# Interleaving the blocks of a recurrent mixer, and moving the head projections of an attention loop

## The chip, the cores and the metric

The kernel runs on the 8 cores of one Trainium2 chip. Each core runs the same program on its own 1024 tokens; the cores do not exchange data. The time is that of the slowest core, in microseconds (us) on the device. A core has a matrix engine (TensorE, PE in the profile), a vector engine (VectorE, DVE), an engine for activation functions (ScalarE, ACT), a general engine (GpSimd, POOL) and a queue engine (SyncE, SP). Each engine works through its own queue in program order, and waits for the others by semaphores.

## The reference

Two trunk layers of a diffusion backbone. The two parts that matter here are the recurrent half of the mixer of layer 0 and the attention of layer 1, cut to what is computed:

```
def rglru_dir(x, wa, ba, wi, bi, lam, h0, reverse):
    r = sigmoid(einsum('blnh,nhk->blnk', xb, wa) + ba)
    i = sigmoid(einsum('blnh,nhk->blnk', xb, wi) + bi)
    log_a = -LRU_C * r * softplus(-lam)
    a = exp(log_a)
    mult = sqrt(-expm1(2.0 * log_a))
    return linear_scan(a, mult * (i * x), h0, reverse)

# even_mixer, its recurrent half
gate, x_b = split(ub, 2)
xc = dwconv(x_b, lru_conv_w, 2, 1) + lru_conv_b
hf = rglru_dir(xc, ..., h0f, False)
hb = rglru_dir(xc, ..., h0b, True)
y_b = (hf + hb) * gelu(gate)

# attend, for each of 8 heads
s = einsum('bqhd,bkhd->bhqk', qi, k) * scale
p = softmax(s)
o = einsum('bhqk,bkhd->bqhd', p, v)
```

## The kernel before

Everything is held feature-major: 128 features on the partitions, the core's 1024 tokens along the free axis, mostly as two halves of 512 (`hh`), which is what one PSUM bank holds in float32. The kernel is written out in order; a small recording layer (`K.op`, `K.mm`, `K.dma`) keeps for every tile the last writer and the readers, and puts a semaphore wait in front of an instruction where one is needed. Nothing reorders: the order of the code is the order of every engine's queue. All matmuls are recorded by one helper and so carry one line, L159; `K.bank()` hands out the eight PSUM banks in rotation and skips those in `K.reserved`. Weights come through `ring`, six slots of SBUF; the loads are issued by POOL (L193).

**The recurrent stage** (L578 to L676) loops over eight blocks `j` of 128 channels. One block is a chain:

- F, the front: `proj` runs 16 matmuls for the gate `gg` and 16 for the input `xb`; ScalarE copies `xb` to `U4` (L589); a tanh form of GELU goes back and forth between ScalarE and VectorE (L594, L595, L597, L599, L600); then a convolution of four taps into `xc`, the first on ScalarE (L604), three on VectorE (L608) and four small corrections (L612); ScalarE writes `xc` out as bf16 `xcb` and halved as `xch` (L618, L619).
- G, the gates: 8 matmuls of `xcb` with `wa` and `wi`, for two directions and two halves, each read by a tanh on ScalarE (L631) into `thr` and `thi`.
- B, the back: for both directions two exponentials of `thr` on ScalarE (L637, L639), two cheap VectorE steps (L643, L645), a Ln and an Exp on ScalarE, which make the square root (L649, L650), two products and a correction on VectorE (L655, L656, L659), a scan (L663 forward, L668 backward), the sum of both and the product with the gate (L674, L675), and two small copies on POOL (L666, L671).

At `j` = 0 and `j` = 4 two weight tiles are loaded, for four blocks each. The tiles `thr`, `thi`, `av`, `a2` and `hd` have one buffer per direction, `U4`, `xc` and `xcb` one, `gl` and `xch` two. ScalarE keeps one table of functions at a time: Tanh and Exp before Ln share one, Ln and the Exp behind it another, and the change between them is an `ACT_TABLE_LOAD`.

**The attention loop** (from L1046) runs over 8 heads. A head begins with 24 matmuls that project its queries and keys (18 from `cqn`, 6 from `ckva`), which ScalarE copies out as `qn` (L1050) and `kn` (L1064) and VectorE turns into `qr` (L1056 to L1058). Then, for each half `hh`, a loop over 12 key tiles: two matmuls for the scores, an Exp on ScalarE into `pT` (L1079), one matmul with `v` and one with ones. The scores go to banks 4 to 7, three tiles ahead. The results lie in banks 0 and 1 for `hh` = 0 and in banks 2 and 3 for `hh` = 1, and are divided on VectorE (L1085, L1086), which sets the banks free.

Of the kernel before, what the change touches and what calls it, by code (L numbers as in the profile page):

```python
# [14 lines left out]
T = 1024  # L15
# [241 lines left out]
def build(stage=99, debug=False):  # L257
# [320 lines left out]
    for j in range(8 if stage >= 3 else 0):  # L578
        if j % 4 == 0:
            pG = ring.load(wview(w_in0, 0, 8, 1536 + (j // 4) * 512, 512), 8, 512)  # L580
            pX = ring.load(wview(w_in0, 0, 8, 2560 + (j // 4) * 512, 512), 8, 512)
# [3 lines left out]
        if not getattr(U, "zeroed", False):  # L585
            K.op(pool, lambda h, U=U: h.memset(U.t[:], 0.0), w=(U,))
            U.zeroed = True
        for hh in range(2):
            K.op(act, lambda h, hh=hh, U=U: h.activation(out=U.t[:, 2 + hh * 512:2 + (hh + 1) * 512], in_=xb[hh].t[:], func=AF.Copy),  # L589
                 r=(xb[hh],), w=(U,))  # L590
        gl = rotbuf("gl", 2, [128, T], F32, MX)
        for hh in range(2):
            sq = rotbuf("gsq", 1, [128, 512], F32, MX)
            K.op(act, lambda h, hh=hh, sq=sq: h.activation(out=sq.t[:], in_=gg[hh].t[:], func=AF.Square), r=(gg[hh],), w=(sq,))  # L594
            K.op(dve, lambda h, sq=sq: h.tensor_scalar(out=sq.t[:], in0=sq.t[:], scalar1=0.044715, scalar2=1.0, op0=ALU.mult, op1=ALU.add),  # L595
                 r=(sq,), w=(sq,))
# [14 lines left out]
        for (ocol, ucol, k) in ((256, 256, 0), (256, 257, 1), (257, 257, 0), (255, 258, 3)):
# [3 lines left out]
                 r=(U, nlcw, xc), w=(xc,))  # L615
        xcb = rotbuf("xcb", 1, [128, T], BF16, MX)
        xch = rotbuf("xch", 2, [128, T], F32, MX)
        K.op(act, lambda h, xc=xc, xcb=xcb: h.activation(out=xcb.t[:], in_=xc.t[:], func=AF.Copy), r=(xc,), w=(xcb,))  # L618
        K.op(act, lambda h, xc=xc, xch=xch: h.activation(out=xch.t[:], in_=xc.t[:], func=AF.Copy, scale=0.5), r=(xc,), w=(xch,))  # L619
        thr_ = [rotbuf("thr", 2, [128, T], F32, MX) for _ in range(2)]  # L620
        thi_ = [rotbuf("thi", 2, [128, T], F32, MX) for _ in range(2)]
        av_ = [rotbuf("av", 2, [128, T], F32, MX) for _ in range(2)]
        a2_ = [rotbuf("a2", 2, [128, T], F32, MX) for _ in range(2)]
        hd_l = [rotbuf("hd", 2, [128, T], F32, MX) for _ in range(2)]
        for d in range(2):
            dj = d * 8 + j
            for (wt, th, hbias) in ((wa, thr_[d], hba), (wi, thi_[d], hbi)):
                for hh in range(2):
# [4 lines left out]
                         r=(b, hbias), w=(th,))  # L633
        for d in range(2):
            dj = d * 8 + j
            thr, av, a2 = thr_[d], av_[d], a2_[d]
            K.op(act, lambda h, thr=thr, av=av, dj=dj: h.activation(out=av.t[:], in_=thr.t[:], func=AF.Exp, bias=m4.t[:, dj:dj + 1], scale=m4.t[:, dj:dj + 1]),  # L637
                 r=(thr, m4), w=(av,))
            K.op(act, lambda h, thr=thr, a2=a2, dj=dj: h.activation(out=a2.t[:], in_=thr.t[:], func=AF.Exp, bias=m8.t[:, dj:dj + 1], scale=m8.t[:, dj:dj + 1]),  # L639
                 r=(thr, m8), w=(a2,))  # L640
        for d in range(2):
            a2 = a2_[d]
            K.op(dve, lambda h, a2=a2: h.tensor_scalar(out=a2.t[:], in0=a2.t[:], scalar1=-1.0, scalar2=1.0, op0=ALU.mult, op1=ALU.add),  # L643
                 r=(a2,), w=(a2,))
            K.op(dve, lambda h, a2=a2: h.tensor_scalar(out=a2.t[:], in0=a2.t[:], scalar1=1e-30, scalar2=None, op0=ALU.max),  # L645
                 r=(a2,), w=(a2,))
        for d in range(2):
            a2 = a2_[d]
            K.op(act, lambda h, a2=a2: h.activation(out=a2.t[:], in_=a2.t[:], func=AF.Ln), r=(a2,), w=(a2,))  # L649
            K.op(act, lambda h, a2=a2: h.activation(out=a2.t[:], in_=a2.t[:], func=AF.Exp, scale=0.5), r=(a2,), w=(a2,))  # L650
        hdir = []
        for d in range(2):
            dj = d * 8 + j
            thi, av, a2, hd = thi_[d], av_[d], a2_[d], hd_l[d]
            K.op(dve, lambda h, a2=a2, xch=xch: h.tensor_tensor(out=a2.t[:], in0=a2.t[:], in1=xch.t[:], op=ALU.mult), r=(a2, xch), w=(a2,))  # L655
            K.op(dve, lambda h, a2=a2, thi=thi: h.scalar_tensor_tensor(out=a2.t[:], in0=thi.t[:], scalar=1.0, op0=ALU.add, in1=a2.t[:], op1=ALU.mult),  # L656
                 r=(a2, thi), w=(a2,))
            c0 = 256 if d == 0 else 255
            K.op(dve, lambda h, av=av, c0=c0: h.tensor_scalar(out=av.t[:, c0:c0 + 513:256], in0=av.t[:, c0:c0 + 513:256], scalar1=flags.t[:, 2:3],  # L659
                                                            scalar2=None, op0=ALU.mult),  # L660
                 r=(av, flags), w=(av,))
            if d == 0:
                K.op(dve, lambda h, av=av, a2=a2, hd=hd, dj=dj: h.tensor_tensor_scan(out=hd.t[:], data0=av.t[:], data1=a2.t[:], initial=h0.t[:, dj:dj + 1],  # L663
                                                                             op0=ALU.mult, op1=ALU.add),
                     r=(av, a2, h0), w=(hd,))
                K.op(pool, lambda h, hd=hd: h.tensor_copy(out=lru_out.t[:, j * 4:(j + 1) * 4], in_=hd.t[:, 255:1024:256]), r=(hd,), w=(lru_out,))  # L666
            else:
                K.op(dve, lambda h, av=av, a2=a2, hd=hd, dj=dj: h.tensor_tensor_scan(out=hd.t[:, ::-1], data0=av.t[:, ::-1], data1=a2.t[:, ::-1],  # L668
                                                                             initial=h0.t[:, dj:dj + 1], op0=ALU.mult, op1=ALU.add),
                     r=(av, a2, h0), w=(hd,))  # L670
                K.op(pool, lambda h, hd=hd: h.tensor_copy(out=lru_out.t[:, 32 + j * 4:32 + (j + 1) * 4], in_=hd.t[:, 0:1024:256]), r=(hd,), w=(lru_out,))  # L671
# [698 lines left out]
```

How the kernel before makes its waits and increments, by code:

```python
    def _waits(self, e, need):  # L119
        for s, v in need.items():
            if e.is_pe and s == e.sem:
                continue
            if e.known.get(s, 0) >= v:
                continue
            e.h.wait_ge(self.sems[s], v)
            e.known[s] = v
# [10 lines left out]
    def op(self, e, fn, r=(), w=(), inc=True):  # L137
        self._waits(e, self._need(r, w))
        ins = fn(e.h)
        if inc:
            e.n += 1
            ins.then_inc(self.sems[e.sem], 1)
            ev = (e.sem, e.n)
        else:
            ev = (e.sem, e.n + 1)
        for t in w:
            t.w = [ev]
            t.r = []
        for t in r:
            self._addr(t, ev)
        return ins
# [57 lines left out]
    def barrier(self):  # L209
        for e in self.engs:
            for f in self.engs:
                if f is e or f.n == 0:
                    continue
                if e.known.get(f.sem, 0) < f.n:
                    e.h.wait_ge(self.sems[f.sem], f.n)
                    e.known[f.sem] = f.n
            for ds in self.dma_sems:
                if e.known.get(ds[0], 0) < ds[1]:
                    e.h.wait_ge(self.sems[ds[0]], ds[1])
                    e.known[ds[0]] = ds[1]
# [1 line left out]
    def finish(self):  # L222
        sp = self.sp
        for f in self.engs:
            if f is sp or f.n == 0:
                continue
            if sp.known.get(f.sem, 0) < f.n:
                sp.h.wait_ge(self.sems[f.sem], f.n)
        for ds in self.dma_sems:
            sp.h.wait_ge(self.sems[ds[0]], ds[1])
        self.es.close()
```

The softmax here doesn't subtract the row's maximum and nothing guards it: scores larger than these inputs give would overflow.

## Time and profile before

| | |
|---|---|
| median of 4 runs | 2883.37 us |
| the profiled execution | 2883.13 us |
| its span on the slowest core, core 0 | 2882.1 us |
| spans of the 8 cores | 2852.6 to 2882.1 us |
| PE busy | 2049.6 us, 71% |
| VectorE busy | 1045.9 us, 36% |
| ScalarE busy | 749.5 us, 26% |
| POOL busy | 168.3 us, 6% |

The table is read so: the span runs from the first instruction to the last, and the profiled execution takes 1.0 us more than it. The shares are means over stages of quite different kind; the recurrent stage lies at 185 to 568 us of the span, the attention loop at 1565 to 1818 us. Between them are the output projection, the dense feed-forward part and the long convolution, behind them the experts.

### The profile page before, as it was taken

The page shows a single profiled execution, that of the slowest core. Times are in us where ns is not written, and L with a number is a line of the kernel's source. Part 1 is how long each engine was busy: PE and PEld are TensorE (multiplying, and loading weights), DVE is VectorE, ACT ScalarE, POOL GpSimd, SP SyncE. Part 2 cuts the span into 40 slices and gives each one's busy share as a digit, 9 for nine tenths or more (in the row PEclk, how much of TensorE's full clock was granted, in tenths as well). Part 3 has the DMA queues.
Part 4 walks back from the last instruction along what each step waited for, and adds up shares of the span by engine and source line. Part 5 has one row for each costly group of instructions (what it writes and reads, how often), then busy time and mean ns, then how long its engine had stood idle before and what let it go on. Part 6 is the DMA issues. An engine that isn't in the chain of part 4 may idle for free.

```text
span 2882.1 us, 27603 instructions; the slowest of 8 cores (2852.6 to 2882.1 us)
## 1 busy us (share of the span) xinstructions
PE 2049.6 (71%) x9394; PEld 883.9 (31%) x9394; DVE 1045.9 (36%) x1460; ACT 749.5 (26%) x1150; POOL 168.3 (6%) x183
## 2 busy tenths in 40 slices
PE   1442222166788944467775888859999999999997
PEld 0221010022233411222222333314444444444443
DVE  1125535532122222455552343234333333343333
ACT  3115544432201044411113555151001011011011
POOL 0100000100001000000000000000000000000000
PEclk9676565587899967778887999979999999999998
DMA  6950020037155923202212000353654564745631
GB/s 118 132 74 0 0 29 0 8 37 117 35 91 79 131 43 59 80 26 70 73 44 45 1 1 1 45 81 50 91 81 60 81 85 57 101 59 82 90 52 59
DMA packets 199176, 170.64 MB, mean 59 GB/s; under 512 B 14091, under 2 KB 184843, under 8 KB 199040
## 3 DMA queue, kind: packets, MB, share of 16 engines
q0 software_dynamic: 176128, 133.70, 33.5%
q1 hardware_dynamic: 22912, 35.18, 3.7%
q8 instruction: 79, 1.29, 0.2%
q14 instruction: 57, 0.47, 0.1%
HBM read 297.02 MB, written 5.54 MB: 105 GB/s over the span
## 4 chain that ended last, share of the span: by engine, by line
PE 62%; DVE 13%; ACT 9%; DMA 8%; issue 6%; POOL 1%; DVEq 0%; ACTq 0%; POOLq 0%; SPq 0%
PE bank L159 62%; DMA ring<-l_w_mod 4%; DMA ring<-l_w_in 2%; DVE xc L608 1%; DVE cvh L919 1%; DVE rec L1085 1%; ACT h L461 1%; DVE Ys L989 1%; DVE sp L987 1%; DVE sp L986 1%; DVE sp L995 1%; DVE a L656 1%; DVE a L655 1%; DVE sp L994 1%; DVE hd L668 1%
## 5 line engine op out<-in xcount | busy, mean ns | idle before, releaser
L159 PE MATMUL bank<-h,ring 128*128 128x512 bf16 (+1 forms) x4400 | 1006.3, 392 | 189.1 <-DMA ring<-l_w_in 138.1
L159 PEld LDWEIGHTS bank<-h,ring 128*128 128x128 bf16 (+1 forms) x4400 | 439.2, 101 | 750.5 <-issue 271.1
L159 PE MATMUL bank<-actt,ring 128*128 128x512 bf16 x1760 | 384.2, 381 | 0.0
L775 ACT ACTIVATE sgt<-bank 128x512 f32<-128x512 f32 x220 | 131.3, 597 | 634.2 <-PE bank L159 634.1
L780 DVE TENSOR_TENSOR sgt<-sgt,bank 128x512 f32<-128x512 f32 x176 | 121.1, 688 | 363.9 <-PE bank L159 363.9
L159 PEld LDWEIGHTS bank<-actt,ring 128*128 128x128 bf16 x1760 | 172.9, 98 | 209.4 <-issue 3.9
L797 DVE SCALAR_TENSOR_TENSOR x<-bank,mod,x 128x512 f32<-128x512 f32 x160 | 120.1, 751 | 259.9 <-PE bank L159 259.9
L159 PE MATMUL bank<-ring,Ys 128*128 128x512 bf16 x512 | 136.9, 414 | 83.6 <-DVE Ys L989 35.9
L159 PE MATMUL bank<-ymix,ring 128*128 128x512 bf16 x640 | 144.3, 389 | 56.9 <-DMA ring<-l_w_out 48.5
L159 PE MATMUL bank<-xcb,wa 128*128 128x512 bf16 x32 | 16.6, 621 | 220.9 <-ACT xcb L618 220.9
L782 DVE TENSOR_TENSOR actt<-sgt,bg 128x512 bf16<-128x512 f32 x176 | 121.9, 692 | 18.7 <-DVE sgt L780 0.5
L1079 ACT ACTIVATE pT<-bank 128x512 bf16<-128x512 f32 x192 | 109.7, 599 | 54.1 <-PE bank L159 52.3
L159 PEld LDWEIGHTS bank<-ymix,ring 128*128 128x128 bf16 x640 | 63.7, 100 | 137.1 <-issue 65.3
L1085 DVE RECIPROCAL rec<-bank 128x512 f32<-128x512 f32 x16 | 53.7, 3357 | 137.7 <-PE bank L159 137.7
L159 PEld LDWEIGHTS bank<-ring,Ys 128*128 128x128 bf16 x512 | 52.1, 102 | 167.9 <-issue 119.6
L777 DVE TENSOR_TENSOR actt<-sgt,bank 128x512 bf16<-128x512 f32 x44 | 30.3, 688 | 190.5 <-PE bank L159 186.7
L443 ACT ACTIVATE sq<-x 128x512 bf16<-128x512 f32 x64 | 35.1, 616 | 208.4 <-PE bank L159 86.7
L1143 ACT ACTIVATE bg<-bank 128x512 bf16<-128x512 f32 x16 | 9.6, 597 | 289.3 <-PE bank L159 288.5
L159 PE MATMUL bank<-qn,kn 128*128 128x512 bf16 x192 | 73.5, 383 | 11.5 <-ACT kn L1064 9.8
L159 PE MATMUL bank<-sq,ones_bf 128*128 128x512 bf16 x90 | 41.7, 515 | 55.7 <-ACT sq L443 32.3
L159 PE MATMUL bank<-qr,kr_all 128*128 128x512 bf16 x192 | 73.5, 383 | 0.8 <-DVE qr L1058 0.8
L159 PEld LDWEIGHTS bank<-xcb,wa 128*128 128x128 bf16 x32 | 3.5, 127 | 229.1 <-issue 229.1
(211 smaller groups left out, 1735.6 us busy)
## 6 DMA issues: line engine op xcount, KB each, us to landing
ring<-l_w_mod POOLq DMA_DIRECT2D x24, 1024.0 KB, 21.0
ring<-l_exp_down POOLq DMA_DIRECT2D x32, 704.0 KB, 7.4
ring<-iFm SPq DMA_DIRECT2D x16, 1024.0 KB, 7.6
ring<-l_exp_gate POOLq DMA_DIRECT2D x16, 1024.0 KB, 8.7
ring<-l_exp_up POOLq DMA_DIRECT2D x16, 1024.0 KB, 10.9
ring<-l_w_in POOLq DMA_DIRECT2D x11, 1024.0 KB, 17.0
ring<-l_w_out POOLq DMA_DIRECT2D x8, 768.0 KB, 14.1
ring<-l_exp_gate POOLq DMA_DIRECT2D x8, 768.0 KB, 7.0
```

Source lines behind the costliest of these rows:

```text
L159: ins = e.h.matmul(out_ap, lhsT, rhs, start=start, stop=stop)
L443: K.op(act, lambda h, c=c, sq=sq: h.activation(out=sq.t[:], in_=X(c, hh), func=AF.Square), r=(xh[c][hh],), w=(sq,))
L461: K.op(act, lambda h, c=c, tmp=tmp, o_ap=o_ap, sh=sh: h.activation(out=o_ap, in_=tmp.t[:], func=AF.Identity, bias=sh, scale=gs_ap(c)), r=( ...
L608: K.op(dve, lambda h, k=k, U=U, xc=xc: h.scalar_tensor_tensor(out=xc.t[:], in0=U.t[:, k:k + T], scalar=lcw.t[:, 8 * k + j:8 * k + j + 1], ...
L655: K.op(dve, lambda h, a2=a2, xch=xch: h.tensor_tensor(out=a2.t[:], in0=a2.t[:], in1=xch.t[:], op=ALU.mult), r=(a2, xch), w=(a2,))
L775: K.op(act, lambda h, hh=hh, sgt=sgt: h.activation(out=sgt.t[:], in_=bgk[hh].t[:], func=AF.Silu), r=(bgk[hh],), w=(sgt,))
L777: K.op(dve, lambda h, hh=hh, sgt=sgt, jj=jj: h.tensor_tensor(out=actt[jj].t[:, HS[hh]], in0=sgt.t[:], in1=buk[hh].t[:], op=ALU.mult), r=(s ...
L780: K.op(dve, lambda h, hh=hh, sgt=sgt: h.tensor_tensor(out=sgt.t[:], in0=sgt.t[:], in1=buk[hh].t[:], op=ALU.mult), r=(sgt, buk[hh]), w=(sgt,))
L782: K.op(dve, lambda h, hh=hh, sgt=sgt, jj=jj: h.tensor_tensor(out=actt[jj].t[:, HS[hh]], in0=sgt.t[:], in1=bg.t[:, HS[hh]], op=ALU.mult), r ...
L797: K.op(dve, lambda h, b=b, oc=oc, hh=hh: h.scalar_tensor_tensor(out=X(oc, hh), in0=b.t[:], scalar=gate_ap(oc), op0=ALU.mult, in1=X(oc, hh) ...
L1079: K.op(act, lambda h, sbk=sbk, pT=pT: h.activation(out=pT.t[:], in_=sbk.t[:], func=AF.Exp, scale=SC), r=(sbk,), w=(pT,))
L1085: K.op(dve, lambda h, rec=rec, db=db: h.reciprocal(out=rec.t[:], in_=db.t[:]), r=(db,), w=(rec,))
```

## The change

Both loops are written out in another order.

In the recurrent stage the body of the loop becomes three functions, `lru_F`, `lru_G` and `lru_B`. `lru_F` and `lru_B` are generators that stop after each recorded instruction; `zipper` takes two steps of F of block `j+1` for each step of B of block `j`, and the rest of B follows when F has ended. Then the gates G of block `j+1` come as one piece. In B every instruction of 1024 columns is split into two of 512, each with its own dependences (`halves`); a scan's second half starts from the last column of the first. F keeps its lengths. All four weight tiles of the stage are loaded at `j` = 0 and held.

In the attention loop the projections become `head_proj`; head 0's come ahead of the loop, and those of head `hd_+1` are recorded in the middle of head `hd_`, behind the key loop of `hh` = 0 and ahead of its division. Meanwhile banks 0 and 1 are reserved.

```diff
-    for j in range(8 if stage >= 3 else 0):
-        if j % 4 == 0:
-            pG = ring.load(wview(w_in0, 0, 8, 1536 + (j // 4) * 512, 512), 8, 512)
-            pX = ring.load(wview(w_in0, 0, 8, 2560 + (j // 4) * 512, 512), 8, 512)
+    pst = {}
+
+    def halves(X):
+        if not hasattr(X, "hv"):
+            X.hv = [Tl(X.t, X.name + "_h0"), Tl(X.t, X.name + "_h1")]
+        return X.hv
+
+    def lru_F(j, out):
+        if j == 0:
+            for h4 in range(2):
+                for k_, c_ in (("pG", 1536), ("pX", 2560)):
+                    pst[k_ + str(h4)] = ring.load(wview(w_in0, 0, 8, c_ + h4 * 512, 512), 8, 512, hold=True)
+        pG, pX = pst["pG%d" % (j // 4)], pst["pX%d" % (j // 4)]
         gg = proj(pG[1], pG[0], (j % 4) * 128)
...
+        out.update({"xcb": xcb, "xch": xch, "gl": gl})
+        yield
+
+    def lru_G(j, st):
+        xcb = st["xcb"]
...
-            K.op(act, lambda h, thr=thr, av=av, dj=dj: h.activation(out=av.t[:], in_=thr.t[:], func=AF.Exp, bias=m4.t[:, dj:dj + 1], scale=m4.t[:, dj:dj + 1]),
-                 r=(thr, m4), w=(av,))
+            for hh in range(2):
+                K.op(act, lambda h, thr=thr, av=av, dj=dj, hh=hh: h.activation(out=av.t[:, HS[hh]], in_=thr.t[:, HS[hh]], func=AF.Exp,
+                                                                            bias=m4.t[:, dj:dj + 1], scale=m4.t[:, dj:dj + 1]),
+                     r=(halves(thr)[hh], m4), w=(halves(av)[hh],))
+                yield
...
-                K.op(dve, lambda h, av=av, a2=a2, hd=hd, dj=dj: h.tensor_tensor_scan(out=hd.t[:], data0=av.t[:], data1=a2.t[:], initial=h0.t[:, dj:dj + 1],
-                                                                             op0=ALU.mult, op1=ALU.add),
-                     r=(av, a2, h0), w=(hd,))
+                K.op(dve, lambda h, av=av, a2=a2, hd=hd, dj=dj: h.tensor_tensor_scan(out=hd.t[:, 0:512], data0=av.t[:, 0:512], data1=a2.t[:, 0:512],
+                                                                                 initial=h0.t[:, dj:dj + 1], op0=ALU.mult, op1=ALU.add),
+                     r=(halves(av)[0], halves(a2)[0], h0), w=(halves(hd)[0],))
+                yield
+                K.op(dve, lambda h, av=av, a2=a2, hd=hd: h.tensor_tensor_scan(out=hd.t[:, 512:1024], data0=av.t[:, 512:1024], data1=a2.t[:, 512:1024],
+                                                                         initial=hd.t[:, 511:512], op0=ALU.mult, op1=ALU.add),
+                     r=(halves(av)[1], halves(a2)[1], halves(hd)[0]), w=(halves(hd)[1],))
+                yield
...
+    def zipper(gF, gB, nf=2, nb=1):
+        aF, aB = gF is not None, gB is not None
+        while aF or aB:
+            for _ in range(nf):
+                if aF:
+                    try:
+                        next(gF)
+                    except StopIteration:
+                        aF = False
+            for _ in range(nb):
+                if aB:
+                    try:
+                        next(gB)
+                    except StopIteration:
+                        aB = False
+    if NJ:
+        stj = {}
+        zipper(lru_F(0, stj), None)
+        lru_G(0, stj)
+        for j in range(NJ):
+            nst = {} if j + 1 < NJ else None
+            zipper(lru_F(j + 1, nst) if nst is not None else None, lru_B(j, stj))
+            if nst is not None:
+                lru_G(j + 1, nst)
+            stj = nst
+        for k_ in pst:
+            pst[k_][0].held = False
     K.dma(sp, lru_d, lru_out.t[:], lru_out, r=(lru_out,))
...
-        for hd_ in range(8):
+        def head_proj(hd_):
...
+            return qn, qr, kn
+
+        nxt = head_proj(0)
+        for hd_ in range(8):
+            qn, qr, kn = nxt
...
+                if hh == 0 and hd_ + 1 < 8:
+                    K.reserved += K.banks[0:2]
+                    nxt = head_proj(hd_ + 1)
+                    del K.reserved[-2:]
                 rec = rotbuf("rec", 2, [128, 512], F32, P4)
```

Three places show what that does to the queues. The first is ScalarE's queue from one block's B to the next block's gates. Before (`a` is `a2`, the trailing numbers are buffers):

```order
L637 ACTIVATE av_87<-thr_83,m_67 128x1024
L639 ACTIVATE a_89<-thr_83,m_68 128x1024
L637 ACTIVATE av_88<-thr_84,m_67 128x1024
L639 ACTIVATE a_90<-thr_84,m_68 128x1024
L649 ACTIVATE a_89<-a_89 128x1024
L650 ACTIVATE a_89<-a_89 128x1024
L649 ACTIVATE a_90<-a_90 128x1024
L650 ACTIVATE a_90<-a_90 128x1024
L589 ACTIVATE U_75<-bank 128x512 x2
L594 ACTIVATE gsq_78<-bank 128x512
L599 ACTIVATE gsq_78<-gsq_78 128x512
```

And of the changed kernel, from the first exponentials of B to the Ln:

```order
L668 ACTIVATE av_87<-thr_83,m_67 128x512
L605 ACTIVATE gsq_78<-bank 128x512
L672 ACTIVATE a_89<-thr_83,m_68 128x512
L613 ACTIVATE gsq_78<-gsq_78 128x512
L668 ACTIVATE av_87<-thr_83,m_67 128x512
L605 ACTIVATE gsq_78<-bank 128x512
L672 ACTIVATE a_89<-thr_83,m_68 128x512
L668 ACTIVATE av_88<-thr_84,m_67 128x512
L613 ACTIVATE gsq_78<-gsq_78 128x512
L672 ACTIVATE a_90<-thr_84,m_68 128x512
L620 ACTIVATE xc_79<-U_75,lcb,lcw 128x1024
```

The GELU steps of the next block (`gsq`) and its first tap (`xc`) now stand between the exponentials of this one; the four Ln and Exp pairs, the next gates and the next copies to `U` follow in this order.

The second is VectorE's queue. Before, the end of one block's back, then the next block's front:

```order
L668 SCALAR_TENSOR_TENSOR hd_92<-av_88,h_60,a_90 128x1024
L674 TENSOR_TENSOR hd_91<-hd_91,hd_92 128x1024
L675 SCALAR_TENSOR_TENSOR ymix_13<-hd_91,gl_76 128x1024
L595 TENSOR_SCALAR gsq_78<-gsq_78 128x512
L597 TENSOR_TENSOR gsq_78<-gsq_78,bank 128x512
L600 SCALAR_TENSOR_TENSOR gl_77<-gsq_78,bank 128x512
```

In the changed kernel the next block's front stands ahead of this block's back; where the one passes into the other:

```order
L625 SCALAR_TENSOR_TENSOR xc_79<-U_75,lcw,xc_79 128x1024 x3
L630 SCALAR_TENSOR_TENSOR xc_79<-U_75,nlcw,xc_79 128x3 x2
L679 TENSOR_SCALAR a_89<-a_89 128x512
L630 SCALAR_TENSOR_TENSOR xc_79<-U_75,nlcw,xc_79 128x3 x2
L682 TENSOR_SCALAR a_89<-a_89 128x512
L679 TENSOR_SCALAR a_89<-a_89 128x512
L682 TENSOR_SCALAR a_89<-a_89 128x512
L679 TENSOR_SCALAR a_90<-a_90 128x512
```

What moved is the convolution (L608 and L612 before), from behind the back of the block before it to a place in front of its L679.

The third place is PE's queue in the middle of a head. Before, the scores of the second half (`qn`, `qr`) follow the last key tile of the first:

```order
L159 MATMUL bank<-pT_248,v_236 128x512
L159 MATMUL bank<-pT_248,ones_bf 128x512
L159 MATMUL bank<-qn_237,kn_239 128x512
L159 MATMUL bank<-qr_223,kr_all 128x512
L159 MATMUL bank<-qn_237,kn_239 128x512
```

Of the changed kernel, the 24 projections of the next head (`cqn`, `ckva`) stand there; their beginning:

```order
L159 MATMUL bank<-pT_248,v_236 128x512
L159 MATMUL bank<-pT_248,ones_bf 128x512
L159 MATMUL bank<-cqn_144,ring_4 128x512
L159 MATMUL bank<-cqn_145,ring_4 128x512
L159 MATMUL bank<-cqn_146,ring_4 128x512
```

They stood behind the last key tile of the second half before; there the next head's scores now follow at once.

## Rows read from the trace of the kernel before

**Rows 1.** The page: its first line.

```profile
span 2882.1 us, 27603 instructions; the slowest of 8 cores (2852.6 to 2882.1 us)
```

**Rows 2.** Two blocks: us, PE, PEld, DVE, ACT, POOL busy (count), PEclk, DMA, GB/s.

```profile
247.30:289.50 42.20, 10.34 (x40) 4.21 (x40) 23.30 (x28) 22.83 (x27) 2.23 (x2) 0.62 0.00 0
...
374.10:437.80 63.70, 19.74 (x72) 7.72 (x72) 22.76 (x28) 24.51 (x30) 3.91 (x4) 0.66 0.24 33
```

**Rows 3.** Waits, 205 to 570 us: total, times, longest.

```profile
PE bank L159 <- ACT xcb L618: 220.9, 8, 32.2
DVE a L643 <- ACT a L639: 85.6, 16, 9.9
...
ACT L599 <- DVE gsq L597: 66.6, 8, 10.6
...
PE bank L159 <- DMA ring<-l_w_in: 35.3, 2, 34.5
```

**Rows 4.** The order of time, blocks 1 and 4: start, length, instruction.

```profile
257.00 1.23 ACT L604 ACTIVATE xc<-U,lcb,lcw 128x1024 f32<-128x1024 f32 x1
...
263.81 1.06 ACT L618 ACTIVATE xcb<-xc 128x1024 bf16<-128x1024 f32 x1 [5.59 <-DVE xc L612]
...
268.29 7.07 PE L159 MATMUL bank<-h,ring 128*128 128x512 bf16 x32
...
387.83 5.19 PE L159 MATMUL bank<-h,ring 128*128 128x512 bf16 x16 [34.54 <-DMA ring<-l_w_in]
...
393.81 3.61 PE L159 MATMUL bank<-h,ring 128*128 128x512 bf16 x16 [0.79 <-DMA ring<-l_w_in]
```

**Rows 5.** The scans' tile: lengths in ns, first and last start.

```profile
L663 DVE TENSOR_TENSOR_SCAN hd<-av,h,a x8: 2350/2351/2352, 240.1 to 557.7; 128x1024 f32<-128x1024 f32 x8
```

**Rows 6.** Instructions by line: busy us, mean ns, idle before them.

```profile
L461 ACT ACTIVATE h<-nt,mod,gs 128x512 bf16<-128x512 f32 x32 | 24.3, 800 | 3.6 <-DVE nt L454 3.6
...
L454 DVE TENSOR_TENSOR nt<-x,rstd 128x512 f32<-128x512 f32 x64 | 41.9, 689 | 64.0 <-ACT rstd L450 55.7 <-ACT h2f L466 8.1
...
L631 ACT ACTIVATE thi<-bank,hbi 128x512 f32<-128x512 f32 x32 | 21.9, 684 | 1.5
...
L637 ACT ACTIVATE av<-thr,m 128x1024 f32<-128x1024 f32 x16 | 19.7, 1230 | 0.0
...
L656 DVE SCALAR_TENSOR_TENSOR a<-thi,a 128x1024 f32<-128x1024 f32 x16 | 19.6, 1226 | 1.8
...
L650 ACT ACTIVATE a<-a 128x1024 f32<-128x1024 f32 x16 | 16.9, 1057 | 1.5
...
L643 DVE TENSOR_SCALAR a<-a 128x1024 f32<-128x1024 f32 x16 | 11.1, 694 | 85.6 <-ACT a L639 85.6
...
L649 ACT ACT_TABLE_LOAD x8 | 10.3, 1283 | 0.1
L599 ACT ACTIVATE gsq<-gsq 128x512 f32<-128x512 f32 x16 | 10.1, 629 | 12.3 <-DVE gsq L597 12.2
...
L595 DVE TENSOR_SCALAR gsq<-gsq 128x512 f32<-128x512 f32 x16 | 6.8, 424 | 52.5 <-ACT gsq L594 52.5
...
L659 DVE TENSOR_SCALAR av<-av,flags 128x3 f32<-128x3 f32 x16 | 3.6, 223 | 0.0
```

**Rows 7.** Attention, same columns: two heads, and the sum of seven.

```profile
1591.69:1625.67 33.98, 28.11 (x120) 11.89 (x120) 12.03 (x11) 16.68 (x29) 0.00 (x0) 0.95 0.00 0
...
1718.91:1748.49 29.58, 26.18 (x120) 11.39 (x119) 11.93 (x10) 16.67 (x29) 0.00 (x0) 1.00 0.00 1
...
sum 222.45, PE 194.87 PEld 83.68 DVE 83.64 ACT 116.93 POOL 0.00; mean PE 27.84 PEld 11.95 DVE 11.95 ACT 16.70 POOL 0.00
```

**Rows 8.** The order of time where the third head begins.

```profile
1625.67 3.36 DVE L1085 RECIPROCAL rec<-bank 128x512 f32<-128x512 f32 x1 [6.21 <-PE bank L159]
...
1629.17 5.80 PE L159 MATMUL bank<-cqn,ring 128*128 128x512 bf16 x18 [3.61 <-DVE rec L1085]
...
1637.73 0.38 PE L159 MATMUL bank<-qn,kn 128*128 128x512 bf16 x1 [1.35 <-ACT kn L1064]
```

More of the change, by code:

```diff
@@ L641, in build @@
         for d in range(2):
             a2 = a2_[d]
[L643 to L646, printed above, removed]
+            for hh in range(2):
+                K.op(dve, lambda h, a2=a2, hh=hh: h.tensor_scalar(out=a2.t[:, HS[hh]], in0=a2.t[:, HS[hh]], scalar1=-1.0, scalar2=1.0, op0=ALU.mult, op1=ALU.add),
+                     r=(halves(a2)[hh],), w=(halves(a2)[hh],))
+                yield
+                K.op(dve, lambda h, a2=a2, hh=hh: h.tensor_scalar(out=a2.t[:, HS[hh]], in0=a2.t[:, HS[hh]], scalar1=1e-30, scalar2=None, op0=ALU.max),
+                     r=(halves(a2)[hh],), w=(halves(a2)[hh],))
+                yield
@@ L647, in build @@
         for d in range(2):
             a2 = a2_[d]
-            K.op(act, lambda h, a2=a2: h.activation(out=a2.t[:], in_=a2.t[:], func=AF.Ln), r=(a2,), w=(a2,))
-            K.op(act, lambda h, a2=a2: h.activation(out=a2.t[:], in_=a2.t[:], func=AF.Exp, scale=0.5), r=(a2,), w=(a2,))
+            for hh in range(2):
+                K.op(act, lambda h, a2=a2, hh=hh: h.activation(out=a2.t[:, HS[hh]], in_=a2.t[:, HS[hh]], func=AF.Ln), r=(halves(a2)[hh],), w=(halves(a2)[hh],))
+                yield
+                K.op(act, lambda h, a2=a2, hh=hh: h.activation(out=a2.t[:, HS[hh]], in_=a2.t[:, HS[hh]], func=AF.Exp, scale=0.5), r=(halves(a2)[hh],), w=(halves(a2)[hh],))
+                yield
@@ new lines, in lru_B @@
+        for d in range(2):
+            thi, av, a2 = thi_[d], av_[d], a2_[d]
+            for hh in range(2):
+                K.op(dve, lambda h, a2=a2, hh=hh: h.tensor_tensor(out=a2.t[:, HS[hh]], in0=a2.t[:, HS[hh]], in1=xch.t[:, HS[hh]], op=ALU.mult),
+                     r=(halves(a2)[hh], xch), w=(halves(a2)[hh],))
+                yield
+                K.op(dve, lambda h, a2=a2, thi=thi, hh=hh: h.scalar_tensor_tensor(out=a2.t[:, HS[hh]], in0=thi.t[:, HS[hh]], scalar=1.0, op0=ALU.add,
+                                                                               in1=a2.t[:, HS[hh]], op1=ALU.mult),
+                     r=(halves(a2)[hh], halves(thi)[hh]), w=(halves(a2)[hh],))
+                yield
+            for (hh, sl) in (((0, slice(256, 257)), (1, slice(512, 769, 256))) if d == 0 else ((0, slice(255, 512, 256)), (1, slice(767, 768)))):
+                K.op(dve, lambda h, av=av, sl=sl: h.tensor_scalar(out=av.t[:, sl], in0=av.t[:, sl], scalar1=flags.t[:, 2:3], scalar2=None, op0=ALU.mult),
+                     r=(halves(av)[hh], flags), w=(halves(av)[hh],))
+                yield
@@ L653, in build @@
             dj = d * 8 + j
[L654 to L661, printed above, removed]
@@ L662, in build @@
[L662 to L671 removed]
+            av, a2, hd = av_[d], a2_[d], hd_l[d]
@@ new lines, in build @@
+    NJ = 8 if stage >= 3 else 0
+    def zipper(gF, gB, nf=2, nb=1):
[13 more added lines that the diff above has]
+                        aB = False
```

51 lines of the change are left out of this document (42 added, 9 removed).

## The prediction, made before the changed kernel ran

> **What bounds the kernel now.** I read the page's head first, then the two loops that the change touches, each by its stretches, its waits and its order of time. The span is 2882.1 us [rows 1]; with the 1.0 us around it, that profiled execution took 2883.1, which is 0.3 under the median of 2883.4, so a saving found in its trace can be taken from either.
>
> In the recurrent stage no engine is full. A block takes 42.2 us, in which VectorE is busy for 23.3, ScalarE for 22.8 and PE for 10.3 [rows 2]. The waits show why: PE sits 220.9 us until `xcb` is there, VectorE 85.6 us for the exponentials, ScalarE 66.6 us for the GELU products that stand behind the scans [rows 3]. So the bound is a chain that goes from engine to engine, F to G to B to the next F, and the next block's front is late only because it stands behind this block's back. The fifth block takes 63.7 us, 21.5 more [rows 2], and PE's longest wait for a weight load, 34.5 us, is there [rows 3, 4]: the load is issued by POOL behind the small copies of the block before. First to last forward scan the stage takes 557.7 - 240.1 = 317.6 us [rows 5], which is six blocks of 42.3 and the long one.
>
> In the attention loop PE is the bound: a head's 120 matmuls take 26.2 busy us at clock 1.00, of a period that averages 222.45 / 7 = 31.8 [rows 7]. The rest is the joint between heads. There PE waits 3.6 us for the division, since the next projections need the banks that it reads, then runs 18 projections in 5.80 us, and waits 1.35 us for `kn` [rows 8].
>
> **The recurrent stage after.** The new order makes two chains, F of block j+1 and B of block j, that share ScalarE and VectorE. I walk one period down ScalarE's queue, with lengths from [rows 6].
>
> Gates: a table load, 1.28, and eight tanh of 0.684: 6.75.
>
> Copies to `U`: PE can start the next projections when the first gate's bank has been read, 0.7 us after the gates begin. It has been idle by then. After a long idle 16 matmuls took 5.19 us, and the next 16 took 3.61 [rows 4]; so the 24 that end the first bank of `xb` take 5.19 + 8 x 0.215 = 6.9. With 0.4 for the hand-over, an estimate, the first copy can begin at 8.0; the gates ended at 5.5, so ScalarE waits 2.5, copies for 0.6, waits 1.1 for the second bank (8 x 0.215 = 1.7 apart) and copies again: 4.8. Behind these copies B's exponentials are queued, so VectorE gets its next work later by as much.
>
> GELU of the next block among six exponentials: an exponential of 512 columns with two pointer operands is not in the trace; the nearest row is L461, of that length and kind, 0.80. So 6 x 0.80 + 2 x 0.6 + 2 x 0.63 = 7.3, and some 0.2 in short waits for VectorE: 7.5.
>
> From the first tap (L604) to `xcb` the trace shows 263.81 - 257.00 = 6.8 [rows 4]; the last two exponentials lie inside, and an interleaved L643 of half length, 0.42, stands in VectorE's way: 7.2. ScalarE idles for over 4 us of it; this wait stays on the path.
>
> `xcb` and `xch`, as L650 without pointers: 2.1. Then a table load and eight Ln and Exp of 512 columns at 0.63, by L599: 6.3.
>
> The sum is 6.75 + 4.8 + 7.5 + 7.2 + 2.1 + 6.3 = 34.7 us against 42.3.
>
> What is late next: VectorE. Behind the first Ln and Exp it has eight products of 0.69, four corrections of 0.22, four half scans, four instructions of 0.69 for sum and output, 14.2 us, and with 1.0 for hand-overs, an estimate, 15.2. It starts 2.5 us into ScalarE's Ln block and ends at 17.7, while ScalarE reaches the next GELU step that needs it at 6.3 + 6.75 + 4.8 + 1.4 = 19.2. So it has 1.5 us in hand. Single buffers leave as little: the gates into the second `thi` stand 11.7 us into this stretch, and the products that read it end at 9.6; the first exponential into `av` stands at 17.9, and the scans end at 15. Half a scan is not in the trace: between 2.35 / 2 = 1.18 with no fixed part and 1.33 with the 0.15 that splitting costs elsewhere (2 x 0.689 - 1.226); I take 1.26. The Trainium skill (VectorE: DVE Perf Modes, section The TRN2 errata) speaks against the splitting: a fixed cost per instruction is paid again by each small tile. By its 150 cycles, an estimate from that page, a half scan would be 1.25, and the sum the same; the trace agrees with its 0.15 per splitting.
>
> The splitting costs on ScalarE 4 x (1.60 - 1.23) + 4 x (1.26 - 1.06) = 2.3 per block, and on VectorE 0.6 in L643 and L645, 0.6 in the products, 0.3 in the scans, 0.3 in the sum, 0.45 in the corrections: 2.3. It is within the sums above.
>
> The stage: between the ends of gates 0 and gates 7 there were 317.6 us and now 7 x 34.7 = 242.9; 74.7 less, 21.5 of it the fifth block's load. All four weight loads now stand at block 0; the two that are needed there are still the first in POOL's queue, and the clearing of `U4`, which they now precede, has until the first of them lands. The last block's B has no front to share with and only the splitting to pay: 3 more. Saved: 72. If the four loads landed in any other order, block 0 would start 6 us later at most by [rows 4], where the second tile came 393.81 - 387.83 behind the first.
>
> **The attention loop after.** At the joint between heads the next scores need nothing that is late, so PE runs on. In the middle of a head 24 matmuls are added; banks 4 to 7 are free by then, since the last Exp is ahead of the last products, and banks 2 and 3 were read by the last head's division, 3.36 and a product long [rows 8], while this head's first half ran. So they start at once, at full clock. The next scores need a bank that the projections used last: either the third `kn` copy or the last `qr` product must be done. That is the wait of 1.35 us [rows 8], which stays; it takes the place of the 3.6 us that go. Period: 120 x 0.215 and 0.2 for a run's end make 26.0, and 26.0 + 1.35 = 27.4. The division of `hh` = 0 now stands behind six `qr` steps on VectorE, but its banks are needed only by the next head. Saved: 222.45 - 7 x 27.4 = 31 us. Bounds: 18, if the clock drops behind each wait as it did behind the 3.6 us (18 matmuls in 5.80 us, 1.9 over 18 x 0.215), and 40 with no wait at all; I take the wait alone, since behind 1.35 us the row at clock 1.00 shows no loss.
>
> 2883.1 - 72 - 31 = **2780 us**.
>
> **Rivals.**
>
> Cold projections, 2816. The granted clock in the stage is 0.62 [rows 2], between the two levels of 1.2 and 2.4 GHz. If the 32 projections ran wholly at 1.2 GHz, they would take 13.7 us, and ScalarE would wait 3.4 us more for the first bank and 1.7 more for the second: 5.1 x 7 = 36 us lost. For it: the gate matmuls now run early, and PE is idle again between them and the projections. Against: 32 projections took 7.07 us behind eight gate matmuls, and even after 34.5 us of idleness the second 16 ran at full speed [rows 4]. The Trainium skill (TensorE: Matmul & The Clock Gate, section HAM oscillation) tells of kernels that start every burst cold; the rows show that for a burst's first part only, which is in my sum.
>
> Nothing gained in attention, 2811. If the projections in the middle cost what the joint did, because the scores must wait for copies that ScalarE and VectorE make late, the 31 us stay. For it: the same `kn` wait; against: 3.6 us of the old joint were the division alone.
>
> VectorE as the bound, 2740. If ScalarE's waits close up, for instance because `xcb` comes earlier, a period falls to VectorE's own work, 23.3 + 2.3 and some 3.4 of hand-overs, an estimate, 29: 7 x 5.7 = 40 us more. Against: the wait at `xcb` is a dependence, not a queue.
>
> No overlap, slower, 2920. In-order queues can undo an interleaving: if each step of F waits for one of B and the reverse, a block costs both chains in series, 42.3 + 4.6 for the splitting + the projections, now in the open and cold, 13.7 less the 5.5 under the gates: 55.1. Then 7 x 12.8 = 90 are lost, 21.5 and 31 gained: +37. It decides from a period of 51 us on ((21.5 + 31 + 9) / 7 above 42.3). For it: ScalarE's order fixes the first tap behind six exponentials. Against: of F's steps only four wait for VectorE within the walk.
>
> **How the numbers follow.** My forecast 0.73, with 2762 to 2800 as its own range; cold projections 0.10; no gain in attention 0.06; VectorE's bound 0.07; no overlap 0.03; 0.01 for mixtures that end near nothing. The range of 8 in 10 takes in the first two rivals and leaves out most of the others: 2752 to 2816. A measurement of this kernel can tell about 0.3%, 9 us, from no change: faster 0.96, within it 0.01, slower 0.03.
>
> **What would show it.** Right: forward scans about 34.7 us apart, all alike; no wait for `l_w_in` after the first block; ScalarE's longest waits at `xcb` (over 4 us a block) and at the first `U` copy (2 to 3 us); two table loads a block; in attention divisions alternately about 10 and 17 us apart and PE's clock at 1.00. Wrong: more than two table loads a block, VectorE with no idle time in a block, or projections of 13 us. A period over 37 or under 32 us breaks the walk.

## The result, and the profile after

The changed kernel takes 2782.85 us (median of 11 runs), the kernel before 2881.3 (median of 16): the ratio is 0.9656 [0.9631, 0.9681]. Forecast were 2780, with 2752 to 2816 as the range. In some executions one die ran at a lower clock; the ratios leave these out, and below a time stands only where they don't distort it.

The page of the profiled execution (2782.53 us) begins so, as in [rows 1]; of before, core 0 was the slowest, now core 5 is:

```profile
span 2781.5 us, 27887 instructions; the slowest of 8 cores (2753.6 to 2781.5 us)
## 1 busy us (share of the span) xinstructions
PE 2048.7 (74%) x9394; PEld 883.5 (32%) x9394; DVE 1055.9 (38%) x1572; ACT 760.9 (27%) x1214; POOL 163.4 (6%) x183
```

PE does the same work; VectorE and ScalarE are busy for 10.0 and 11.4 us more, which is the splitting. Spans of single cores say little about a stage: the part between the two loops differs by up to 11.5 us on a core, either way, with nothing changed in it. So from here on two stages are read on each core, and their median over the cores is given: the recurrent stage from the start of the first copy to `U` to that of the last product with the gate, and attention from the start of the first `qn` copy to that of the last product of a division.

| us | recurrent stage | attention |
|---|---|---|
| before | 360.0 (357.5 to 361.6) | 247.3 (246.3 to 250.3) |
| after | 287.4 (287.2 to 289.2) | 219.9 (219.9 to 220.1) |
| difference | -72.6 | -27.4 |

The two differences sum to 100.0, the medians differ by 98.5. All that follows of rows is core 0, as before.

**The recurrent stage.** One block, in the columns of [rows 2], where it took 42.20:

```profile
293.81:328.71 34.90, 12.65 (x41) 4.57 (x40) 24.60 (x43) 24.31 (x37) 1.69 (x2) 0.65 0.00 0
```

Still no engine is full. The waits of the stage, 205 to 500 us (total, times, longest), against [rows 3]:

```profile
PE bank L159 <- ACT xcb L637: 132.0, 8, 16.8
DVE gsq L607 <- ACT gsq L605: 56.1, 16, 22.4
ACT xcb L637 <- DVE xc L630: 36.2, 8, 5.6
PE bank L159 <- ACT thr L654: 34.7, 6, 5.9
ACT U L599 <- PE bank L159: 33.4, 15, 4.4
```

PE's wait for `xcb` fell from 220.9 to 132.0, VectorE's 85.6 for the exponentials are gone, and no weight load is waited for. What ScalarE now waits for is what the walk named: `xcb` and the copies to `U`. Where one period went is seen in the order of time (start, length, instruction, wait in brackets). ScalarE's queue in the period of that row, with PE's start of the projections:

```profile
291.33 1.28 ACT L654 ACT_TABLE_LOAD   x1
292.62 1.27 ACT L654 ACTIVATE thr<-bank,hba 128x512 f32<-128x512 f32 x2
293.46 9.08 PE L159 MATMUL bank<-h,ring 128*128 128x512 bf16 x32 [5.89 <-ACT thr L654]
296.06 1.30 ACT L654 ACTIVATE thi<-bank,hbi 128x512 f32<-128x512 f32 x2
300.90 0.60 ACT L599 ACTIVATE U<-bank 128x512 f32<-128x512 f32 x1 [3.54 <-PE bank L159]
302.69 0.60 ACT L599 ACTIVATE U<-bank 128x512 f32<-128x512 f32 x1 [1.18 <-PE bank L159]
303.18 0.80 ACT L668 ACTIVATE av<-thr,m 128x512 f32<-128x512 f32 x1
310.86 1.22 ACT L620 ACTIVATE xc<-U,lcb,lcw 128x1024 f32<-128x1024 f32 x1
317.82 1.06 ACT L637 ACTIVATE xcb<-xc 128x1024 bf16<-128x1024 f32 x1 [4.32 <-DVE xc L630]
319.84 1.28 ACT L688 ACT_TABLE_LOAD   x1
326.23 1.28 ACT L654 ACT_TABLE_LOAD   x1
```

The forward scans, where [rows 5] had them 42.3 apart, by their tile,

```profile
L711 DVE TENSOR_TENSOR_SCAN hd<-av,h,a x8: 1272/1275/1275, 258.2 to 484.4; 128x512 f32<-128x512 f32 x8
```

and the last three of them in the order of time:

```profile
431.80 1.27 DVE L711 TENSOR_TENSOR_SCAN hd<-av,h,a 128x512 f32<-128x512 f32 x1
466.33 1.27 DVE L711 TENSOR_TENSOR_SCAN hd<-av,h,a 128x512 f32<-128x512 f32 x1
484.42 1.27 DVE L711 TENSOR_TENSOR_SCAN hd<-av,h,a 128x512 f32<-128x512 f32 x1
```

The first six distances are 33.9 to 35.7, 34.70 in the mean ((466.33 - 258.16) / 6); the last is 18.1.

**Attention.** The divisions of the first two heads, two each, and the first of the third:

```profile
1502.52 3.34 DVE L1187 RECIPROCAL rec<-bank 128x512 f32<-128x512 f32 x1
1512.99 3.36 DVE L1187 RECIPROCAL rec<-bank 128x512 f32<-128x512 f32 x1 [6.33 <-PE bank L159]
1530.08 3.34 DVE L1187 RECIPROCAL rec<-bank 128x512 f32<-128x512 f32 x1
1540.14 3.36 DVE L1187 RECIPROCAL rec<-bank 128x512 f32<-128x512 f32 x1 [5.92 <-PE bank L159]
1557.24 3.34 DVE L1187 RECIPROCAL rec<-bank 128x512 f32<-128x512 f32 x1
```

They stand 10 and 17 us apart in turn; a head takes 27.56 and 27.16, the next two together 54.79 at clock 1.00, where [rows 7] had single heads of 29.58 and 33.98. What is left of the joint of [rows 8] is a wait in the middle of a head, of two kinds in turn:

```profile
1502.36 0.38 PE L159 MATMUL bank<-qn,kn 128*128 128x512 bf16 x1 [1.35 <-ACT kn L1157]
1529.52 0.38 PE L159 MATMUL bank<-qn,kn 128*128 128x512 bf16 x1 [0.87 <-DVE rt L1150]
```

### The profile page after: what moved, and what is told of

The parts are those of the page before. It is cut to its first block, busy times and chain, and to the rows that moved or that the text cites. A ratio compares the mean times of both kernels' runs of the same rounds, so it can differ in the third digit from the quotient of the medians.

```text
span 2781.5 us, 27887 instructions; the slowest of 8 cores (2753.6 to 2781.5 us)
## 1 busy us (share of the span) xinstructions
PE 2048.7 (74%) x9394; PEld 883.5 (32%) x9394; DVE 1055.9 (38%) x1572; ACT 760.9 (27%) x1214; POOL 163.4 (6%) x183
## 4 chain that ended last, share of the span: by engine, by line
PE 65%; DVE 12%; ACT 8%; DMA 8%; issue 5%; POOL 1%; DVEq 0%; ACTq 0%; SPq 0%; POOLq 0%
PE bank L159 65%; DMA ring<-l_w_mod 4%; DMA ring<-l_w_in 1%; DVE xc L625 1%; DVE cvh L1012 1%; ACT h L461 1%; DVE Ys L1082 1%; DMA ring<-l_ffn_up 1%; DVE sp L1080 1%; DVE sp L1079 1%; DVE sp L1088 1%; DVE sp L1087 1%; DMA ring<-l_w_out 1%; ACT zs L1073 1%; ACT a L688 1%
## 5 line engine op out<-in xcount | busy, mean ns | idle before, releaser
L159 PE MATMUL bank<-xcb,wa 128*128 128x512 bf16 x32 | 16.6, 620 | 132.0 <-ACT xcb L637 132.0
L159 PE MATMUL bank<-pT,v 128*128 128x512 bf16 x192 | 72.8, 379 | 0.0
L159 PE MATMUL bank<-pT,ones_bf 128*128 128x512 bf16 x192 | 72.8, 379 | 0.0
```

Source lines behind the costliest of these rows:

```text
L159: ins = e.h.matmul(out_ap, lhsT, rhs, start=start, stop=stop)
```

## The experiments

Theory A is the prediction's, and in the later runs what the earlier ones had made of it. At first it says: a chain that goes from engine to engine bounds the recurrent stage, the interleaving shortens it by laying F beside B, the load is a stall of its own, and attention gains its joint apart from all that. First the change is taken to pieces.

**Each half alone.** The first kernel has the new recurrent stage and the old attention, the second the reverse.

> The changed recurrent stage with the attention loop as it was before. Theory A, the two parts are independent and each is worth what the walk gave it: the stage's 72 us go, the attention's 27 to 31 us do not, so about 2881 - 72 = 2809 us. Rival B, the parts share something (the time saved in the first stage is given back later as a weight wait, or the attention part carries more than its stage shows): under 2795 or over 2825 us.

> The changed attention loop with the recurrent stage as it was before. Theory A: the joint between heads shrinks from about 31.3 us a head to 27.4, so 27 to 31 us go: about 2852 us. Rival B, nothing gained in attention: the wait in the middle of a head takes the place of the old one, 2881 us; and then the first experiment would have shown the whole 98.

Measured: 2811.63 us, 0.9749 [0.9705, 0.9793], stages 287.3 and 249.7; and 2853.37, 0.9903 [0.9872, 0.9933], stages 359.5 and 219.9. Each stage moves with its own half and not with the other's (249.7 lies among the 246.3 to 250.3 of the kernel before). There is one more thing in the first half than splitting, interleaving and loads: in `lru_B` VectorE's products of both directions stand ahead of the first scan, where before each direction's products stood in front of its own scan.

**The load alone**: the kernel before, with all four loads at block 0.

```diff
-        if j % 4 == 0:
-            pG = ring.load(wview(w_in0, 0, 8, 1536 + (j // 4) * 512, 512), 8, 512)
-            pX = ring.load(wview(w_in0, 0, 8, 2560 + (j // 4) * 512, 512), 8, 512)
+        if j == 0:
+            ...
+                    pst[k_ + str(h4)] = ring.load(wview(w_in0, 0, 8, c_ + h4 * 512, 512), 8, 512, hold=True)
```

> The kernel before with one edit alone: all four weight tiles of the recurrent stage are loaded at block 0 and held. Theory A: the fifth block falls from 63.7 to 42.3 us and nothing else moves: 21 us less, about 2860 us. Rival B: the four loads share the queues so that block 0 starts later, by 6 us or more, and 15 us or less is left: 2866 us or more.

Measured: 2857 to 2863 us, 0.9924 [0.9896, 0.9952]; the stage 339.7, so the load is worth 20.3 us of the 72.6.

**The reverse**: the changed kernel, with the second pair loaded at block 4 as before (`if j % 4 == 0` in place of `if j == 0`).

> The changed kernel, but with the second pair of weight tiles loaded at block 4, where it was loaded before the change. Theory A: the load is issued by POOL behind the small copies of an earlier block, so one block again waits for it, and with two chains in flight the projections come as late: 15 to 21 us more, about 2800 us. Rival B: now that the front runs a block ahead, the load is issued early enough and is hidden: under 2788 us, and the 21 us of the hoist alone are no term of the sum.

Measured: the stage 306.6, 19.2 more than after; the ratio 0.9793 [0.9732, 0.9855]. In the stage the load costs in the new order what it cost in the old. The times, 2802 to 2822 us, are 20 to 40 us above the changed kernel's; the traced run is the fastest, and where the others spent 12 and 20 us more no trace shows. PE's waits for the load:

```profile
PE bank L159 <- DMA ring<-l_w_in: 23.1, 2, 22.3
```

**No interleaving**: the split instructions and the hoisted loads stay, but B runs ahead of F.

```diff
-            zipper(lru_F(j + 1, nst) if nst is not None else None, lru_B(j, stj))
+            zipper(None, lru_B(j, stj))
+            zipper(lru_F(j + 1, nst) if nst is not None else None, None)
```

> The changed kernel, but with the whole of B of a block recorded ahead of F of the next, so that nothing is interleaved; the halves, the hoisted loads and the attention loop stay. Theory A: the interleaving is what shortens a block, and the halves cost time where nothing covers them: a block of 42.3 plus 1 to 3 us, no load stall: the stage ends 60 to 75 us later than with the interleaving, 2845 to 2858 us. Rival B, the halves themselves let VectorE and ScalarE of one block overlap and give most of the gain: a block of under 39 us, under 2815 us.

Measured: the stage 347.7, 60.3 more than after, the ratio 0.9858 [0.9813, 0.9902]; the times, 2839 and 2843 us, lie just under A's. The old waits are back, in nearly the sizes of [rows 3]:

```profile
PE bank L159 <- ACT xcb L637: 242.6, 8, 32.9
DVE a L679 <- ACT a L672: 76.3, 32, 8.2
ACT L613 <- DVE gsq L610: 74.6, 8, 10.8
```

So the 72.6 us come apart as: the load -20.3 (339.7 - 360.0), the splitting, with VectorE's new order of products and scans in it and nothing beside it, +8.0 (347.7 - 339.7), the interleaving -60.3 (287.4 - 347.7).

**What the splitting is worth**: the interleaving stays, B is recorded in instructions of 1024 columns as before. With the width two things go back: VectorE's old order of products and scans, and in the gates the two halves of a `thr` or `thi` count as one tile.

> The changed kernel with the back B left in instructions of 1024 columns, as before the change; interleaving, hoisted loads and attention stay. Theory A, ScalarE's queue is the chain and every split instruction on it is paid: four exponentials of 1.23 for eight of 0.80, four Ln and Exp of 1.06 for eight of 0.63, and B has half as many steps, so that the next block's first tap (xc) stands behind fewer exponentials, under which the wait at xcb is then hidden less or more: 3 to 4 us a block less, about 25 us less in all, 2758 us. Rival B, the halves are needed for the overlap, since VectorE can start on the first half sooner: a block gets longer, 2790 us or more.

Measured: 2758.75, 0.9586 [0.9551, 0.9621], the stage 257.7. The halves, with those two things, cost 29.7 us of the stage: the change is better without its splitting. No run parts the three. ScalarE's wait at `xcb`, 36.2 in the changed kernel, is here

```profile
ACT xcb L637 <- DVE xc L630: 24.0, 8, 5.6
```

**How many steps of F go with one of B.** One in place of two (`nf=1`), with the halves, and with full width:

> The changed kernel with one step of F for each step of B in place of two. Theory A: the exposed wait at xcb (4.3 us a block) is there because ScalarE's queue has nothing left to do while VectorE convolves; with half the pace the Ln and Exp pairs stand ahead of xcb and the wait is filled: a block of 31 to 32 us in place of 34.7, with still two table loads, and 20 us less: 2762 us. Rival B: xcb comes later, so the gates of the next block wait for it, and nothing or less than nothing is gained: 2780 us or more.

> The same pace of one to one with B in instructions of 1024 columns: now a tanh of F's GELU falls between the Ln and Exp steps of B. Theory A: this breaks the grouping by function table, there are four table loads a block in place of two, and each costs its 1.28 us and holds the queue: a block of 38 to 40 us, slower than the changed kernel by 20 to 35 us, about 2810 us. Rival B: a table load is hidden under the waits of ScalarE, and the time is that of the full width at two to one, about 2758 us.

Measured: with the halves 2753 to 2780 us, 0.9616 [0.9502, 0.9729], the stage 262.9, 24.5 less than after; with full width 2817.37, 0.9802 [0.971, 0.9894], the stage 320.1, 62.4 more than at full width and two to one. The runs of both scatter by 28 us; by its times the first can't be told from the changed kernel, by the stage on eight cores (259.6 to 263.4) it can. In the first, ScalarE's two waits shrink from 33.4 and 36.2:

```profile
ACT U L599 <- PE bank L159: 25.4, 14, 4.4
...
ACT xcb L637 <- DVE xc L630: 22.1, 8, 5.6
```

Together 22.1 of the 25.9 that core 0 gains. In the second the order puts a GELU tanh between a Ln and its neighbours, and ScalarE changes tables four times a block:

```profile
L683 ACT ACT_TABLE_LOAD x15 | 19.2, 1283 | 0.3
L613 ACT ACT_TABLE_LOAD x8 | 10.3, 1283 | 1.6 <-DVE gsq L610 1.5
L654 ACT ACT_TABLE_LOAD x7 | 9.0, 1283 | 0.1
```

These 30 loads are 14 more than the changed kernel's 16, 18 us; the rest of the 62.4 is a chain that closes less well: ScalarE's wait at `xcb` is 79.3 there, against 24.0. Half-width steps two to one and full-width steps one to one are thus both wrong, in opposite directions: what counts is how much of B, in us, goes with how much of F.

**The wait at `U` taken away**: the projections of block `j+2` are recorded ahead of the gates of block `j+1`, in banks 0 to 3, the gates in banks 4 to 7.

```diff
-            zipper(lru_F(j + 1, nst) if nst is not None else None, lru_B(j, stj))
-            if nst is not None:
-                lru_G(j + 1, nst)
+            zipper(lru_F(j + 1, sts[j + 1]) if j + 1 < NJ else None, lru_B(j, sts[j]))
+            if j + 2 < NJ:
+                lru_P(j + 2, sts[j + 2])
+            if j + 1 < NJ:
+                lru_G(j + 1, sts[j + 1])
```

> The changed kernel (halves, two to one), with the projections of a block put ahead of the gates of the block before in PE's queue, in four banks of their own, and the gates in the other four; so they need not wait for the gates' banks. Theory A: ScalarE's waits at the two U copies go (3.2 + 1.2 us a block in the trace of the changed kernel), but VectorE has only 1.5 us in hand and becomes the bound: about 2 us a block, 15 us in all, 2768 us. Rival B: the whole wait is on the path, 4.4 us a block, 30 us in all, 2753 us.

Measured: 2757 to 2763 us, 0.9578 [0.9558, 0.9599]; the recurrent stage 270.6, 16.8 less than after, where A had 15. A's reason, that VectorE has little in hand, shows too. Of the 33.4 us at `U`, 1.5 are left once the stage runs; but ScalarE's wait for VectorE's product ahead of the GELU tanh, 7.0 in the changed kernel, is now

```profile
ACT gsq L618 <- DVE gsq L615: 20.8, 8, 3.3
```

But the time was 5 to 11 us below A's, because attention, which was not touched, took 214.7 in place of 219.9. A had no reason for that; it is followed up last.

**Early projections with full width:**

> The early projections and the full width of B together, the rest as in the changed kernel. Theory A: the full width gives ScalarE and VectorE room, so that the wait at the U copies is now on the path nearly whole: a block of about 28 us, 45 to 50 us less than the changed kernel, 2735 us. Rival B: the two overlap (the full width has taken what the early projections would give): 2750 us or more.

Measured: 2723.06 us (2717 to 2729), 0.946 [0.9441, 0.9479], stages 235.0 and 214.7. It beats both kernels; A had 45 to 50 us, and the recurrent stage alone gives 52.4. One block, and the waits of the stage:

```profile
276.96:304.20 27.24, 13.04 (x40) 4.23 (x40) 22.63 (x28) 22.82 (x28) 2.23 (x2) 0.69 0.00 1
```

```profile
ACT U L604 <- PE bank L159: 28.3, 2, 27.2
ACT xcb L642 <- DVE xc L635: 23.9, 8, 5.6
```

But for the very first one (27.2, for the stage's first weights) the wait at `U` is down to 1.1 us, that at `xcb` to 23.9, and the period falls to 27.24, of which both ScalarE and VectorE are busy for over 22.6.

**Where attention's 5.2 us came from.** The early projections leave the rotation of banks two places further. The changed kernel with that alone:

```diff
+        K.bank_i = 3
         nxt = head_proj(0)
```

> The changed kernel with one line more: the rotation of the PSUM banks is set to bank 3 ahead of head 0's projections in the attention loop (it stood at 1 there; at 3 in the two kernels with the early projections). Nothing else is changed. A, the bank theory: in the changed kernel the middle projections of heads 1, 3, 5 and 7 end in bank 4 with the third kn tile and those of heads 2, 4 and 6 use bank 4 for the last swapped query product, and the next score, which goes to bank 4, waits for its reader, 1.35 us and 0.87 us each (8.0 us in all). From bank 3 on, bank 4 holds the first kn tile or the second rotary product, read long before: waits of at most 0.3 us, and the attention stage falls from 219.9 to about 214.7 us on every core; the recurrent stage stays at 287.4; the whole at about 2778. B, the rival: the 5.2 us came from something else that the early projections did; the stage stays at 219.9 and the waits of 1.35 and 0.87 us stay.

Measured: 2777.18 us in one run; the recurrent stage 287.2, attention 215.6 on every core within 0.1. The waits of 1.35 and 0.87 us in the middle of the heads are gone; of that place this is left, three times:

```profile
1538.09 0.38 PE L159 MATMUL bank<-qn,kn 128*128 128x512 bf16 x1 [0.28 <-DVE rt L1149]
```

From the product of the first division to that of the last it takes 190.3 us, with the early projections 190.3 and 190.5, in the changed kernel 195.6: the bank explains the 5.2 us. (The waits between these two products were 6.7 us and are 0.8; the other 0.6 us is not accounted for.) The stage shows 4.3 of the 5.2, because its beginning, from the first `qn` copy to the first of these products, grew from 24.3 to 25.3 us. The jump from bank 1 to 3 leaves out two banks, so head 0 begins on one that a copy of `v` was still reading; the kernels with the early projections have no such jump and no such wait:

```profile
1487.93 4.21 PE L159 MATMUL bank<-cqn,ring 128*128 128x512 bf16 x18 [1.07 <-ACT v L1136]
```

## Why the prediction was right, step by step

**The bound** was read rightly: a chain, not an engine. Undone, the interleaving gives back 60.3 us and the old waits; done, it takes 7.3 us off a period (42.20 to 34.90) in which both engines are busy for longer than before.

**The walk** gave 34.7 us, and the row above has 34.90, but two of its terms were off against each other. By term, predicted and measured from one start to the next on ScalarE: gates 6.75, 6.03 (291.33 to 297.36); copies to `U` 4.8, 5.82; GELU among exponentials 7.5, 7.68; first tap to `xcb` 7.2, 6.96; `xcb` and `xch` 2.1, 2.02; table, Ln and Exp 6.3, 6.39. PE behaved as said: it started 0.8 us after the first gate, and the first copy came 7.44 later, against 6.9 + 0.4. What was mis-sized is the gates: I took eight full lengths of 0.684, but in the changed kernel they start 0.57 apart. So ScalarE is done earlier and waits longer at `U`, 3.54 where I said 2 to 3; the sum doesn't change, since the copy waits for PE. A term in front of a wait can be wrong at no cost. Why they start closer the kernel of full width shows, whose gates differ in one thing, that both halves of a `thr` are recorded as one tile, so that the second tanh carries a wait for the first. Its pair, and that of the changed kernel:

```profile
316.56 1.47 ACT L654 ACTIVATE thr<-bank,hba 128x512 f32<-128x512 f32 x2
```

```profile
327.52 1.27 ACT L654 ACTIVATE thr<-bank,hba 128x512 f32<-128x512 f32 x2
```

From the ends of gates 0 to those of gates 7 the stage took 317.6 us before (229.15 to 546.74) and now 243.9 (226.02 to 469.88), where the walk had 242.9; the last block's tail grew by 1.7 (21.1 to 22.8), where I had 3, and the first front is 0.8 shorter, as its gates are. Counted to the end of the last product, that is the 72.8 of core 0.

**The load**: 21.5 predicted, 20.3 alone and 19.2 undone in the changed kernel. The 6 us by which block 0 might have started later were not seen: the first copy to `U` starts at 204.3 us before and at 204.5 after, in the median of the cores.

**The splitting**: the halves of a scan took 1.275 and 1.284 forward, 1.259 and 1.284 backward, against 1.26. The busy time per block rose by 1.5 on ScalarE (24.31 - 22.82 at full width) and 2.0 on VectorE (24.60 - 22.63), where I had 2.3 for each. But its price was not the busy time, 1.5 to 2.3 a block: it was some 4 us, 29.7 over the stage. The reason that fits is that a step of B became half as long, so that at two to one F has only half as much of B beside it: at one to one, where the amounts are those of full width and two to one again, the halves, with VectorE's order in them, cost 5.2 over the stage (262.9 against 257.7). The walk went down the real order, so the forecast didn't suffer; the sentence that puts the splitting at 2.3 did.

**Scans all alike**: not so. The last B has no front beside it, and its scan came 18.1 us behind the one before. The sum was counted from gates to gates, where it holds; as a sign to look for, the scans were the wrong mark for the last block.

**VectorE 1.5 us in hand**: its wait in front of the next GELU step was 2.48. It was not the bound, here or at full width; it became late when the wait at `U` went and the halves stayed, and ScalarE's waits for it rose by 13.8 us over the stage (20.8 - 7.0).

**Attention**: the period was 27.4 as forecast (27.56 and 27.16), its wait of 1.35 and its clock of 1.00 too. The saving was 27.4, not 31, and this is the largest miss. What failed is the number it was taken from: 222.45 us for seven heads is that of core 0, whose attention took 250.3, the longest of the eight cores; their median was 247.3. On core 0 itself 30.4 were saved. And the 1.35 came only at every other head, with 0.87 at the others. That the forecast time is off by 2.9 us and the forecast saving by 4.6 (103 against 98.5) is luck in part: the median before now stands at 2881.3, 2 us under the time that the 103 were taken from.

**The rivals.** Cold projections: the 32 took 9.08 us, neither the 7.07 they took behind eight gates nor 13.7. VectorE as the bound: no, the period would have been 29. Nothing gained in attention: the half alone gained 27.4. No overlap: the period is 34.90, not 55; even with B recorded ahead of F it stayed at 43.1, and the stage below that of the kernel before, since the hoisted load came with it.

## What to carry over

Where no engine is full and each waits in turn, walk one period down the fullest in-order queue and sum its work and its waits: that was within 1%, and its waits (at `U`, at `xcb`) were a list of what to do next. The stage went down by another 52.4 us, though 29.7 of them came with the full width, for which the walk had 2.3 a block. An interleaving is set by how much of each chain lies side by side, so its ratio and the grain of its steps must be chosen together, and a split that only makes finer steps is to be tried against the whole. A saving per core is taken from the median of the cores, not from the one that ended last.

## What was not expected of the hardware

- The place where a rotation of PSUM banks stands is worth 5.2 us of 220: from one start PE's next score goes to a bank that has not been read out yet, and waits 1.35 or 0.87 us at each head; from another that bank was read earlier, and 0.28 us at every other head are left. Which bank it is was counted from the kernel's own rotation; the trace names the reader that PE waits for.
- On ScalarE a tanh that waits for the one just before it costs 0.2 us more than one that doesn't: a second tanh of 512 columns starts 0.78 us behind the first if both write one tile (1.47 less the 0.69 of one), 0.58 if each half counts as its own (1.27 less 0.69). Four of them a block make 0.8 us, which recording the halves apart gave back in the gates.
- After the change the two stages agree over the eight cores to 2.1 and 0.2 us (before, to 4.1 and 4.0), while the unchanged part between them takes from 982 to 1004 us on the cores of one execution, and moves by up to 11.5 us on a core from the one execution to the other.
